# Sample attention: V as whole rows without a ones column, denominators from kept probabilities, and query rows stored in four copies

## The reference

```
def mem_attend(u, k, v, w_q, w_o):
    q = jnp.einsum('btd,de->bte', u, w_q).reshape(b, t, MEM_HEADS, MEM_HEAD_DIM)
    s = jnp.einsum('bthd,bnhd->bhtn', q, k).astype(jnp.float32) * (MEM_HEAD_DIM ** -0.5)
    p = jax.nn.softmax(s, axis=-1).astype(v.dtype)
    o = jnp.einsum('bhtn,bnhd->bthd', p, v).reshape(b, t, d)
    return jnp.einsum('btd,de->bte', o, w_o)

def trunk(...):
    for i in range(DEPTH):                       # 2 layers
        x = x + mixer(rmsnorm(x))                # pooling in layer 0, short conv in layer 1
        x = x + mem_attend(rmsnorm(x), mem_k[i], mem_v[i], w_q[i], w_o[i])
        x = x + sq_relu_mlp(rmsnorm(x), w_up[i], w_down[i])
```

## Time and profile before

| | us |
|---|---|
| the three runs | 1846.87, 1837.81, 1590.81 (median 1837.81) |
| the profiled execution | 1602.11 |
| its span on the slowest core (core 4) | 1600.6 |
| spans of the 8 cores in it | 1582.9 to 1600.6 |
| PE busy | 1536.1 (96%) |
| DVE, ACT, POOL busy | 874.4, 547.5, 114.1 |

### The profile page before, as it was taken

The page is one execution under the profiler, slowest core; times in us unless marked ns, Lnnn a source line. Parts: engine busy times, 40 slices in busy tenths (PEclk is TensorE's granted clock), DMA queues, the critical chain, the costliest instruction groups (busy, mean ns, idle before and its releaser), DMA issues.

```text
span 1600.6 us, 28149 instructions; the slowest of 8 cores (1582.9 to 1600.6 us)
## 1 busy us (share of the span) xinstructions
PE 1536.1 (96%) x10069; PEld 884.2 (55%) x10076; DVE 874.4 (55%) x2000; ACT 547.5 (34%) x1004; POOL 114.1 (7%) x245
## 2 busy tenths in 40 slices
PE   3899999999999999999999999997999999999996
PEld 3875555555565665555555555553555555555554
DVE  5756774754443344446567665774555444444456
ACT  4756445532112121231223325542653112111342
POOL 2002211110000000000000001220110000000000
PEclk9999999999999999999999999998999999999999
DMA  8978996776637506246000009995674562000013
GB/s 226 218 123 160 182 194 140 143 130 106 96 69 124 96 1 106 32 75 111 1 1 1 1 6 149 174 204 110 125 172 64 108 106 53 1 1 1 12 75 128
DMA packets 96884, 153.05 MB, mean 96 GB/s; under 512 B 5966, under 2 KB 49230, under 8 KB 96732
## 3 DMA queue, kind: packets, MB, share of 16 engines
q0 software_dynamic: 67568, 84.08, 35.4%
q1 hardware_dynamic: 27084, 66.32, 14.7%
q10 hardware_dynamic: 2096, 0.85, 0.2%
HBM read 220.29 MB, written 14.42 MB: 147 GB/s over the span
## 4 chain that ended last, share of the span: by engine, by line
PE 86%; DVE 5%; DMA 4%; issue 2%; ACT 2%; POOL 0%; DVEq 0%; ACTq 0%; SPq 0%; POOLq 0%
PE PS L293 83%; DVE MEM L328 3%; PE PS L297 3%; DMA MEM<-cv 2%; ACT MEM L320 1%; DMA MEM<-gv 1%; DVE MEM L332 1%; DMA MEM<-x 1%; ACT MEM L309 0%; DVE MEM L346 0%; DVE MEM L340 0%; PE PS L302 0%; POOL MEM L355 0%; DVEq L1448 0%; ACT PS L320 0%
## 5 line engine op out<-in xcount | busy, mean ns | idle before, releaser
L293 PE MATMUL PS<-MEM 128*128 128x416 bf16 (+6 forms) x8885 | 1464.0, 325 | 8.8 <-DVE MEM L332 3.6
L293 PEld LDWEIGHTS PS<-MEM 128*128 128x128 bf16 (+1 forms) x8892 | 828.1, 98 | 634.7 <-issue 35.7
L332 DVE TENSOR_TENSOR MEM<-PS,MEM 128x416 f32<-128x416 f32 (+6 forms) x563 | 315.4, 575 | 323.8 <-PE PS L293 253.2
L320 ACT ACTIVATE MEM<-PS 128x416 f32<-128x416 f32 (+5 forms) x475 | 241.8, 510 | 566.6 <-PE PS L293 556.8
L332 DVE TENSOR_TENSOR MEM<-MEM 128x416 bf16<-128x416 f32 (+3 forms) x322 | 184.8, 585 | 276.3 <-ACT MEM L320 265.9
L320 ACT ACTIVATE MEM<-MEM 128x416 bf16<-128x416 f32 (+13 forms) x249 | 175.4, 716 | 179.9 <-DVE MEM L332 156.9
L328 DVE SCALAR_TENSOR_TENSOR MEM<-MEM 128x416 bf16<-128x416 f32 (+9 forms) x370 | 201.7, 597 | 59.8 <-ACT MEM L320 49.9
L297 PE MATMUL PS<-MEM 128*128 128x128 bf16 (+7 forms) x1136 | 75.9, 266 | 32.3 <-DMA MEM<-cv 10.7
L305 DVE SCALAR_TENSOR_TENSOR MEM<-MEM 128x256 f32<-128x256 f32 x256 | 90.7, 418 | 5.0 <-DMA MEM<-qrows 5.0
L297 PEld LDWEIGHTS PS<-MEM 128*128 128x128 bf16 (+3 forms) x1136 | 51.3, 102 | 57.0 <-issue 55.9
L344 ACT COPY MEM<-PS 128x512 f32<-128x512 f32 (+3 forms) x73 | 39.1, 536 | 121.7 <-PE PS L293 107.8
(11 more groups left out here) (25 smaller groups left out, 80.9 us busy)
## 6 DMA issues: line engine op xcount, KB each, us to landing
MEM<-ck SPq DMA_DIRECT2D x64, 512.0 KB, 8.7
MEM<-cv POOLq DMA_DIRECT2D x64, 256.0 KB, 10.7
MEM<-w_down POOLq DMA_DIRECT2D x6, 2048.0 KB, 17.5
MEM<-x SPq DMA_DIRECT2D x16, 512.0 KB, 13.7
MEM<-w_kv POOLq DMA_DIRECT2D x4, 2048.0 KB, 18.5
MEM<-w_o POOLq DMA_DIRECT2D x4, 2048.0 KB, 22.9
MEM<-w_up POOLq DMA_DIRECT2D x32, 256.0 KB, 20.8
MEM<-qrows SPq DMA_DIRECT2D x32, 256.0 KB, 10.6
```

Of the source, the lines that this page charges most:

```text
L293: P.add(PE, "c", lambda e, o=out.ap, l=lhsT.ap, r=rhs.ap: e.matmul(out=o, lhsT=l, rhs=r, start=start, stop=stop), [lhsT, rhs], [out])
L320: P.add(ACT, "c", lambda e, o=out.ap, i=in_.ap: e.activation(out=o, in_=i, func=func, bias=bias, scale=sc), rd, [out])
L332: P.add(eng, "c", lambda e, o=out.ap, a=in0.ap, b=in1.ap: e.tensor_tensor(out=o, in0=a, in1=b, op=op), [in0, in1], [out])
```

## The change

V is loaded as whole rows: the tiles are [2, 1024], there is no memset, and the load of each half is 128 rows of 1024. The 8 matmuls of a sample are 256 columns wide. The denominators come at the end: `SE` writes the probabilities a second time, into `PALL` (8 x 16 columns, in the place of `OTS`), and `fin_a` begins with 8 matmuls of `PALL` with one column of ones, into a bank of the rotation. The query rows are stored four times in DRAM, and each of four loads puts a copy on 32 partitions.

```diff
-    q_d = nc.dram_tensor("qrows", [2, NS, D], BF16, kind="Internal").ap()
+    q_d = nc.dram_tensor("qrows", [2, NQC, NS, D], BF16, kind="Internal").ap()
...
+    PALL = T(OTS.off, BF16, [8, NS])
...
-        VSU = [su.alloc(BF16, [2, 4, 258]) for _ in range(2)]
+        VSU = [su.alloc(BF16, [2, D]) for _ in range(2)]
...
-            qst.append(dma(SP, DV(q_d[l]), QS(p=(0, NS)), "qst"))
+            for r in range(NQC):
+                qst.append(dma(SP, DV(q_d[l, r]), QS(p=(0, NS)), "qst"))
...
         def SDQ(b):
-            dma(SP, (QBU if b < n_att else QBA)[b % 2](), DV(q_d[l, b:b + 1, :].broadcast_to([128, D])), f"qb{b % 2}", after=tuple(qst))
+            w = 128 // NQC
+            for r in range(NQC):
+                dma(SP, (QBU if b < n_att else QBA)[b % 2](p=(r * w, (r + 1) * w)), DV(q_d[l, r, b:b + 1, :].broadcast_to([w, D])), f"qb{b % 2}", after=tuple(qst))
...
             for x in range(2):
-                memset(v(x, sl(0, 4), sl(256, 257)), 1.0, eng=POOL)
-                dma(POOL, v(x, sl(0, 4), sl(0, 256)), DV(cv_d[l, b, x * 128:(x + 1) * 128, :].rearrange("p (h e) -> p h e", h=4)), f"v{nm}{b % 2}")
+                dma(POOL, v(x), DV(cv_d[l, b, x * 128:(x + 1) * 128, :]), f"v{nm}{b % 2}")
...
             act(PBZ[b % 2](sl(0, 8), b), SS(b % 4), AF.Exp, scale=1.0 / 16.0)
+            act(PALL(sl(0, 8), b), SS(b % 4), AF.Exp, scale=1.0 / 16.0)
...
-                    mmx(V(PS[32 * h:32 * h + NS, OBK, 0:257], PSv(OBK, 0, 1).ivs, True), PBZ[b % 2](x * 4 + h),
-                        VS[b % 2](x, h, sl(0, 257)), b == 0 and x == 0, b == NS - 1 and x == 1)
+                    mmx(V(PS[32 * h:32 * h + NS, OBK, 0:256], PSv(OBK, 0, 1).ivs, True), PBZ[b % 2](x * 4 + h),
+                        VS[b % 2](x, sl(h * 256, (h + 1) * 256)), b == 0 and x == 0, b == NS - 1 and x == 1)
...
         def fin_a():
+            bk = nxt()
+            for x in range(2):
+                for h in range(4):
+                    mmx(V(PS[32 * h:32 * h + NS, bk, 0:1], PSv(bk, 0, 1).ivs, True), PALL(x * 4 + h), ONESB(sl(0, 1)), x == 0, x == 1)
...
-                recip(RDS(p=p), pv(256, 257))
+                recip(RDS(p=p), V(PS[p[0]:p[1], bk, 0:1], PSv(bk, 0, 1).ivs, True))
```

More of the change, by code:

```diff
@@ L35 @@
 N_ATT_S = (7, 8)
+NQC = 4
 class V:
@@ L955, in attn_phase @@
         QBA = [QBU[0], T(VWO.off + 2 * 4160, BF16, [D])]
-        VSA = [T(VWO.off + i * 4160, BF16, [2, 4, 258]) for i in range(2)]
+        VSA = [T(VWO.off + i * 4160, BF16, [2, D]) for i in range(2)]
         WOS = T(WQK.off, BF16, [NCH, D])
```

## The result

The change makes the kernel 4.3% slower: the ratio to the kernel before is 1.0428, with an interval of 1.0297 to 1.0559. It compares 1660.72 and 1665.54 us with 1590.81 and 1598.93 us of the kernel before; the median of the four runs of the kernel after is 1668.98 us. Some executions of either kernel are longer, up to 1820 us and more, with a lower clock on the cores of one die, which is why the medians given for the kernel before (1837.81, later 1718.37) are not its undisturbed time, and the ratios here leave such runs out. The profiled execution took 1660.72 us, with a span of 1659.2 on core 0, against 1602.11 and 1600.6 on core 4.

The account below looks back on a forecast made before the run. PE was taken as the bound, busy 1536.1 of 1600.6 us. Chained query loads added +23, +10, +28 and +2, total +63, so 1665 on 1602.11, taken as 1660 for V's relief; range 1605 to 1750.

Parts of the forecast that it names:

- the forecast's scale: Whole kernel: 1660 us, on the scale of the profiled execution (1602.11) and lowest run (1590.81), not the median of 1837.81.
- The sum: Both layers: +23 and +10 us in layer 0, +28 and +2 in layer 1 (attention, MLP), total +63.
- The mechanism: SP's queue: four query loads wait one for another, delaying next keys, DVE's dots, ACT's exponential and PE; slower at 0.72.
- The signs: Traces: some 96 SP waits, 300 us or more; DVE's query wait 50 or more; SBs 18 apart; V wait gone.
- The start: Layer 0's first samples: keys of sample 1 still go out at 150.45 us and SB(1) stays, path 25.4, slack 5.4.
- The first quarter: First query load behind 1 MB of keys: lands in 9 us in attention parts, 5.3 and 3.5 in MLP parts.
- The later quarters: Query loads after the first: 3.5 us each in attention parts, 3.0 in MLP parts, ends 2.4 and 6.9.
- The relief: V as whole rows: a twentieth of DMA time in two stretches; with the V stall gone, 1602 − 12 = 1590.
- the zero for the second exponential: ACT: 32 more exponentials of 226 ns, 7.2 us in all, hidden behind the ones PE needs, so nothing.
- The light chain: Rival on SP's query loads: later quarters land in 2.4 us, attention cycle 16.2, time 1623; chance 0.14.
- the heavy one: Rival on SP's query loads: later quarters take 5 us, 4 in MLP parts, time 1749; chance 0.20.
- the hidden one: Rival on SP's query loads: cycle within 12.6 us, chain hidden, V stall gone, time 1590; chance 0.11.

Follow-up runs that it names:

- Experiment 1: Against the changed kernel, the four query loads of a sample go out without waiting for each other; 1.0002 of the kernel before, median 1599.94 us.
- experiment 2: The kernel before with only the query part added (four copies, four loads each waiting for the one before); 1.0421 of the kernel before, median 1670.56 us.
- experiment 7: The changed kernel with eight query copies and eight chained loads instead of four; 1.1829 of the kernel before, median 1890.33 us.
- experiment 3: The changed kernel without its query part (one query row, one 256 KB load); 0.997 of the kernel before, median 1594.82 us; second time 0.9955.

## What the prediction had right, and the step that failed

**The step that failed is the last one, the forecast's scale.** The sum, +63 us for the chain less some 5 for V, was laid on the profiled execution's 1602.11 and gave 1660. The time on record for the kernel before was the median of 1837.81, and the prediction said of the 236 us between them only that nothing in the profiled execution explains them. Set beside 1837.81 its 1660 is a gain of 10%, while its chances say slower at 0.72: the number and the argument point opposite ways. What the runs showed in its place is a loss of 4.3%, 1660.72 and 1665.54 beside 1590.81 and 1598.93. The 236 us were no part of the kernel: in the later comparisons the runs of the kernel before that the ratios use lie at 1593 to 1604. A forecast has to be of one kind with the time that it is set beside, or be given as a ratio; as +58 on 1602, +3.6%, this one would have been on the right side and near.

**The mechanism was right.** The forecast of slower came from the three waits in a sample's query loads, with keys behind them, DVE's dots behind these and PE's banks behind DVE. Experiment 1 takes the waits away and nothing else, and the loss is gone; experiment 2 adds them alone, and it is there. The signs came too: 96 waits of SP with 376.9 us, DVE's wait at 117.4, the wait for V gone. The SBs are not 18 us apart, though; they come in pairs, 16.2 us each on average in layer 0 and 15.5 in layer 1 (core 0).

**The size of the sum was near by luck.** Forecast +63 on the span; it was +58.6 between the two slowest cores, 69.2 on core 0. By parts, forecast and core 0: attention of layer 0, 23 and 24; MLP of layer 0, 10 and 13; attention of layer 1, 28 and 33 (the forecast was against core 4, whose 10 us stall it counted as covered, and core 0 had none there); MLP of layer 1, 2 and 0. But within layer 0's attention part two terms were off by 11 to 12 us each and cancelled, as the next two paragraphs show.

**The start** was put at nothing without a reason. The sum let the keys of sample 1 go out at 150.45 as before, with SB(1) where it was. The chain of sample 0 stands ahead of them; its four issues lasted from 141.29 to 160.4, with landings of 7.30, 6.38 and 4.96 us between them, and the first two SBs were 12.0 us late already (2.4 of it from a later store):

```profile
141.29 19.14 SPq L357 DMA_DIRECT2D MEM<-qrows  x4
160.52 2.74 SPq L357 DMA_DIRECT2D MEM<-ck  x4
```

In layer 1 the sum counted the chain of sample 0 and had SB(1) 5 us late; it was 13.3 later than by the lag that layer 0 left. That chain was quick (its three landings had means of 2.0 to 2.5 us), so the lateness is not its own; where it comes from is left open.

**The first quarter** was taken at 9 us. Its means in the attention parts are 6.8 and 7.4 us, its medians 5.7 and 5.9, single ones 4.1 to 13.9. So SP's cycle there was 16.4 and 16.6 us instead of 18.4, and the five samples of layer 0 added 11.9 us instead of 23. Those medians are within the 6 us that the prediction had named as a sign of being wrong, and the loss came all the same: with 14.1 and 14.3 us of landings in place of 16, the cycle is still well over PE's 12.6. In the MLP parts 5.3 and 3.5 us were forecast, and the means are 5.5 and 4.8.

**The later quarters** were taken at 3.5 and 3.0 us. The means of the second and third are 3.4 to 3.8 us in the attention parts and 2.8 to 3.4 in the MLP parts, so the term was right; single ones ran from 1.8 to 9.0, wider than the rows of 2.4 and 6.9 that were its ends.

The Trainium skill ("DMA: Bandwidth & Descriptors", "Anatomy of one DMA — SWDGE (gpsimd) path") gives a fixed cost of about 2.0 us per DMA, and it gives it for DMAs that POOL issues, while the query loads are SP's. This case's trace agrees for the quickest quarters alone, with 1.8 us; the 32 KB parts of experiment 7 have a median of 2.0. With it the prediction's sum came to 15 and would have missed most of the loss.

**V and the denominators.** The relief was put at 12 us with the stall gone; it is 5 to 7 (experiment 3). The stall was read off the slowest core alone. The others waited 0 to 9.5 us before, so the bound moved on to cores which had less to win. (The clock's part of the stall is also a little smaller than stated: 19% of 18.10 us is 3.4, not 3.8.) The saving in packets was as worked out: 67,568 − 42,992 = 24,576. Nothing in experiment 3 speaks against the zero for the second exponential, the 16 new matmuls and the memsets.

**The rivals.** The light chain (1623), the heavy one (1749) and the hidden one (1590) did not come; experiment 1, with the waits away, is at 1600. By its own terms the heavy chain's cycle is 1.76 + 9 + 10 + 0.6 = 21.4 us, not 21.9, and its time some 6 us less; nothing hangs on that.

## What to carry to other kernels

When a load is split into pieces, read the waits of the pieces, not only their sizes: a dependency tracker that doesn't know partitions turns four parallel transfers into a chain, on the issuing engine's queue, and everything behind it waits as well. Add up what one queue must do in a round, landings that it waits for included, and set it against the time in which the bound engine consumes a round; below or near it a chain costs little (two parts: 1%), above it the landings are paid for (four parts: 4%, eight: 18%). The Trainium skill ("DMA: Bandwidth & Descriptors", "Rules for kernel authors") advises one transfer of 128 partitions rather than two to halves of them. The runs agree: even with no wait between them, four parts (and four stores) gave 1.0002 where one gave 0.997 on the same chip.

State a forecast as a ratio to a time that you name, above all where the runs of the kernel before disagree among themselves.

## What the runs showed of the hardware

- A 64 KB load landed later where the keys came on another queue at the same time: the second and third quarters had means of 3.8 and 3.6 us in layer 0's attention part with the keys held back, 4.9 and 5.0 with keys coming from POOL's queue; in layer 1's 3.6 and 3.4 against 3.9 and 4.1.
- A DMA written as four pieces per row, adjacent at both ends, ran with the packets of whole rows (42,992 on POOL's queue); with a gap of 4 bytes between the pieces' destinations it took 67,568.
- Keys issued from POOL instead of SP gave 0.9936 (0.9919 to 0.9954), beside 0.9955 (0.994 to 0.9971) for the same kernel with keys on SP on the same chip. The intervals overlap, so a gain is not shown; a loss, which I had thought possible for keys behind POOL's waits for PE, is not there either.
